# A further tile of an expert's tokens, placed between the main products of the next expert by an If/Else

## What is computed

```python
s = jax.nn.sigmoid((t @ w_router).astype(jnp.float32))      # 384 tokens x 16 experts
... top group of 4 experts by its two best scores, top 2 experts inside it, weights w normalised
hid = jax.nn.silu(jnp.einsum('td,edf->tef', t, w_gate)) * jnp.einsum('td,edf->tef', t, w_up)
hid = hid * gates.astype(hid.dtype)[:, :, None]
out = jnp.einsum('tef,efd->td', hid, w_down)                # D = 1024, d_ff = 512
```

## Time and profile before

| | us |
|---|---|
| median of three runs | 1125.43 (1115.67 to 1126.11) |
| span of the profiled execution | 1121.9 |
| PE busy | 982.3 (88%) |
| DVE busy | 404.9 (36%) |
| ACT busy | 157.1 (14%) |
| POOL busy | 123.3 (11%) |
| read from HBM / written | 305.88 MB / 21.30 MB |

### The profile page before, as it was taken

How to read it: one execution, slowest core, us unless ns; L and a number is a source line. 1 busy time by engine, 2 the same in 40 slices (tenths; PEclk the granted TensorE clock), 3 DMA queues, 4 the chain that set the end, 5 groups by cost and what they waited for, 6 DMA issues and landing times. The chain is left out here.

```text
span 1121.9 us, 12453 instructions
## 1 busy us (share of the span) xinstructions
PE 982.3 (88%) x4812; PEld 467.2 (42%) x4812; DVE 404.9 (36%) x902; ACT 157.1 (14%) x364; POOL 123.3 (11%) x188
## 2 busy tenths in 40 slices
PE   4799999997898989988799979999678997889886
PEld 2555545454333333333266544554523333333332
DVE  0189855245211110111435994533521111011206
ACT  1101233220000000000130014422000000000010
POOL 1001200511000000000221020060200000000010
PEclk9899889997999999988799997999579999999988
DMA  9928973368999996999950475225965999999932
GB/s 339 383 95 310 302 298 108 124 219 355 424 420 425 425 367 272 422 427 421 360 220 24 150 270 223 76 92 185 362 234 220 415 426 425 423 424 422 420 134 75
DMA packets 64570, 328.59 MB, mean 293 GB/s; under 512 B 7448, under 2 KB 10184, under 8 KB 48084
## 3 DMA queue, kind: packets, MB, share of 16 engines
q1 hardware_dynamic: 44224, 277.89, 61.6%
q0 software_dynamic: 9072, 27.89, 6.8%
q10 hardware_dynamic: 11172, 21.42, 5.8%
HBM read 305.88 MB, written 21.30 MB: 292 GB/s over the span
## 5 line engine op out<-in xcount | busy, mean ns | idle before, releaser
L1782 PE MATMUL ps<-big 128*64 128x512 f32 x1024 | 244.6, 630 | 27.6 <-issue 11.9
L1798 PE MATMUL ps<-big,scr 128*64 128x512 f32 x624 | 156.3, 644 | 5.6 <-DVE scr L1428 4.3
L1477 PE MATMUL ps<-big 128*128 128x384 f32 (+2 forms) x448 | 147.9, 492 | 5.1 <-ACT big L786 5.1
L1782 PEld LDWEIGHTS ps<-big 128*64 128x64 f32 x1024 | 78.5, 144 | 173.1 <-issue 159.5
L1124 DVE SCALAR_TENSOR_TENSOR scr<-scr,convw 128x384 f32<-128x384 f32 x240 | 134.1, 613 | 2.3
L1441 DVE TENSOR_TENSOR scr<-ps,scr 128x256 f32<-128x256 f32 x32 | 13.6, 424 | 278.2 <-ACT scr L953 278.1
L1477 PEld LDWEIGHTS ps<-big 128*128 128x128 f32 x448 | 86.0, 193 | 64.7 <-issue 24.8
L1798 PEld LDWEIGHTS ps<-big,scr 128*64 128x64 f32 x624 | 50.6, 148 | 97.9 <-issue 96.9
L1698 PE MATMUL ps<-big 128*128 128x512 f32 x192 | 84.4, 594 | 1.4 <-ACT big L826 1.4
L1493 PE MATMUL ps<-big,cs_rep 128*32 128x256 f32 x640 | 49.5, 466 | 14.4 <-DMA big<-in_w_mod_dram 14.4
L953 ACT ACTIVATE scr<-ps 128x256 f32<-128x256 f32 x32 | 12.3, 383 | 325.2 <-PE ps L1782 325.2
(11 more groups left out here) (231 smaller groups left out, 842.5 us busy)
## 6 DMA issues: line engine op xcount, KB each, us to landing
big<-in_w_gate_dram SPq DMA_DIRECT2D x32, 2048.0 KB, 18.4
big<-in_w_up_dram SPq DMA_DIRECT2D x32, 2048.0 KB, 22.8
big<-in_w_down_dram SPq DMA_DIRECT2D x32, 2048.0 KB, 18.9
big<-in_w_mod_dram SPq DMA_DIRECT2D x23, 2048.0 KB, 15.3
big<-in_w_in_dram SPq DMA_DIRECT2D x6, 2048.0 KB, 23.5
expert_rows<-scr ACTq DMA_DIRECT2D x68, 128.0 KB, 8.5
big<-in_w_out_dram SPq DMA_DIRECT2D x4, 2048.0 KB, 19.8
expert_rows<-x ACTq DMA_DIRECT2D x1, 7168.0 KB, 42.6
```

The lines of the kernel that those rows point to most:

```text
L1477: mm = pe.matmul(out, stationary(k), moving(k), start=(k == 0), stop=(k == n - 1))
L1782: mm = pe.matmul(ps[b * TT:(b + 1) * TT, bank, :].rearrange("p (m n) -> p m n", m=2), tokens(k), w[:, :, k, b * HF:(b + 1) * HF], start=(k ...
L1798: mm = pe.matmul(ps[b * TT:(b + 1) * TT, bank, :], src[:, k % 2 * P + k // 2 * TT:k % 2 * P + (k // 2 + 1) * TT], w[:, k, b * SEG:(b + 1) ...
```

## The change

On every engine a further tile of expert e-1 moves into the step of expert e. The step is one If/Else on the number of tokens of e-1. In the If arm the tile's operations stand between the main ones; the Else arm holds the main ones alone. So the main operations stand in the program twice.

- PE, If arm: loop for tiles 2 to 5 (`far`), transposes of the tile, main gate/up of e, gate/up of the tile, main down of e-1, next `xT`, hidden transposes of the tile, of e, down of the tile.
- ACT and DVE follow in the same order. POOL gathers the tiles 2 to 5 first, then tile 1.
- Gate and up slots of e-1 are signalled by the first two matmuls of the main down (If) or of the main gate/up of e (Else); the down slot by a small matmul behind the tile's down (If) or the first hidden transpose of e (Else). ACT waits for a new semaphore `y_ps` of `down_main`.
- Experts 14 and 15 have arms of their own. With a further tile of 15, ACT and DVE take the main hidden rows of 15 and the first picked rows ahead of the tile's; without one the order is the old one. The sum with 15's further tile (`sums_15b`) stands behind all products.
- `ov_xsT_free` is new: it tells POOL that the second buffer of the last picked rows is free, where it waited for the copy of the tile's result (`ov_taken`).

The core of the diff, PE:

```diff
-                def expert(e):
...
-                    if past(g0):
-                        pe.wait_ge(hid_ready, g0)
...
-                    gate_up(GU, e, lambda k: hT[i % 2][:, k, j * TT:(j + 1) * TT]).then_inc(gu_ps, 1)
...
-                    if 0 < e < E - 1:
-                        down_main(e - 1)
-                    if j and e + 1 < E:
-                        pe.wait_ge(gathered[(i + 1) % 2], (l * (E // 4) + (i + 1) // 2 + 1) * 16)
-                        xT(i + 1)
-                    pe.wait_ge(hid_ready, g0 + 1)
-                    hidden_transposes(hid, HT).then_inc(hidT_ps, 1)
-                    if e < E - 1:
-                        overflow(pe, n, run, ov_at)
-                    for m in ("g", "u"):
-                        idle_matmul(OV_GU).then_inc(slot_used[slot_of((m, l, e))], 1)
+                for e in range(1, E - 1):
+                    n = tokens_of(pe, e - 1)
+                    with pe.If(n > TT):
+                        if e == 1:
+                            pe.wait_ge(last_taken, l + 1)
+                        far(e - 1, n)
+                        more_transposed(e - 1)
+                        gate_up_main(e)
+                        more_gate_up(e - 1)
+                        down_main(e - 1, slots_gu(e - 1))
+                        next_xT(e)
+                        more_hidden()
+                        hidden_main(e)
+                        more_down(e - 1)
+                        release(("d", l, e - 1))
+                    with pe.Else():
+                        gate_up_main(e, slots_gu(e - 1))
+                        if e == 1:
+                            pe.wait_ge(last_taken, l + 1)
+                        down_main(e - 1)
+                        next_xT(e)
+                        hidden_main(e, slot_used[slot_of(("d", l, e - 1))])
+                n = tokens_of(pe, E - 2)
+                with pe.If(n > TT):
+                    far(E - 2, n)
+                    more_transposed(E - 2)
+                    down_main(E - 2)
+                    more_gate_up(E - 2)
+                    more_hidden()
+                    more_down(E - 2)
+                    release(("g", l, E - 2))
+                with pe.Else():
+                    down_main(E - 2)
+                    release(("g", l, E - 2))
...
+                n = tokens_of(pe, E - 1)
+                with pe.If(n > TT):
+                    loaded(("g", l, E - 1))
+                    loaded(("u", l, E - 1))
+                    far(E - 1, n)
+                    more_transposed(E - 1)
+                    gate_up_main(E - 1)
+                    more_gate_up(E - 1)
+                    hidden_main(E - 1)
+                    pe.wait_ge(y_taken, l * E + E - 1)
+                    sums_14(0)
+                    more_hidden()
+                    down_main(E - 1)
+                    more_down(E - 1)
+                with pe.Else():
+                    gate_up_main(E - 1)
+                    pe.wait_ge(y_taken, l * E + E - 1)
+                    sums_14(0)
+                    hidden_main(E - 1)
+                    down_main(E - 1)
```

DVE for experts 1 to 14, and ACT and DVE for expert 15 with a further tile:

```diff
+                    with dve.If(n > TT):
+                        far_(e - 1, n)
+                        more_x()
+                        hid_of(e)
+                        more_hid(e - 1)
+                        if e % 2:
+                            take_xT(e // 2 + 1)
+                        more_hidT()
+                        hidT_of(e)
...
+                with act.If(n > TT):
+                    far(E - 1, n)
+                    sigmoid_of(E - 1)
+                    scale_pick(l, 0)
+                    scale_pick(l, 1)
+                    more_sigmoid(E - 1)
+                    take_y(E - 1)
+                    scale_pick(l, 2)
+                    more_y_kept()
...
+                    hid_of(E - 1)
+                    add_picked(l, 0)
+                    more_hid(E - 1)
+                    hidT_of(E - 1)
+                    more_hidT()
+                    add_picked(l, 1)
```

The new order of POOL, and its wait:

```diff
                     with pool.If(n > TT):
-                        run(1)
                         with pool.If(n > 2 * TT):
                             for t in range(2, NT):
                                 run(t)
-                        pool.reg_add(ov_at, ov_at, 0)
+                        run(1)
...
-                            pool.wait_ge(ov_taken if n else ov_x_free, asked)
+                            pool.wait_ge(ov_xsT_free if n else ov_x_free, asked)
```

More of the change, by code:

```diff
@@ new lines, in more_y_kept, with row_of, far @@
+                def more_y_kept():
+                    act.wait_ge(ov_y, act.snap(ov_at))
+                    a.copy(ov_y15, ps[:, OV, :]).then_inc(ov_taken, 1)
+                    act.reg_add(ov_at, ov_at, 1)
+                    act.reg_add(ov_next, ov_next, 1)
+                def row_of(e):
+                    return act.value_load(count[0:1, E + e:E + e + 1], min_val=E, max_val=E + MORE - NT + 1)
+                def far(e, n):
+                    def run(t):
+                        row = row_of(e)
+                        more_sigmoid(e)
+                        more_y(t, row)
+                    far_tiles(act, n, run, ov_at)
@@ new lines, in _ @@
+                sigmoid_of(0)
+                act.wait_ge(last_ps, l + 1)
+                for to, bank in ((T15, 6), (T14, OV), (T15b, OV_GU)):
+                    ins = a.copy(to.rearrange("p t n -> p (t n)"), ps[:, bank, 0:TILES * P])
+                ins.then_inc(last_taken, 1)
+                for e in range(1, E - 1):
+                    n = tokens_of(act, e - 1)
+                    with act.If(n > TT):
+                        far(e - 1, n)
+                        row = row_of(e - 1)
+                        sigmoid_of(e)
+                        more_sigmoid(e - 1)
+                        take_y(e - 1)
+                        more_y(1, row)
+                    with act.Else():
+                        sigmoid_of(e)
+                        take_y(e - 1)
@@ new lines, in _ @@
+                n = tokens_of(act, E - 2)
+                with act.If(n > TT):
+                    far(E - 2, n)
+                    row = row_of(E - 2)
+                    take_y(E - 2)
+                    more_sigmoid(E - 2)
+                    more_y(1, row)
+                with act.Else():
+                    take_y(E - 2)
+                n = tokens_of(act, E - 1)
+                with act.If(n > TT):
+                    far(E - 1, n)
[6 more added lines that the diff above has]
+                    more_y_kept()
@@ new lines, in more_hidden, with more_down, far, run @@
+                def more_hidden():
+                    pe.wait_ge(ov_hid_ready, pe.snap(ov_at))
+                    hidden_transposes(ov_hid, OV).then_inc(ov_hT, 1)
+                def more_down(e):
+                    loaded(("d", l, e))
+                    pe.wait_ge(ov_hidT_ready, pe.snap(ov_at))
+                    down(OV, e, ov_hidT).then_inc(ov_y, 1)
+                    pe.reg_add(ov_at, ov_at, 1)
+                    pe.reg_add(ov_count, ov_count, 16)
+                def far(e, n):
+                    def run(t):
+                        more_transposed(e)
+                        more_gate_up(e)
+                        more_hidden()
+                        more_down(e)
+                    far_tiles(pe, n, run, ov_at)
```

285 lines of the change are left out of this document (141 added, 144 removed).

## The result

| | before | after |
|---|---|---|
| median | 1124.13 us (1115.67 to 1126.11) | 1141.64 us (1138.14 to 1142.34) |
| ratio to before, 95% | 1 | 1.0181 (1.0139 to 1.0222) |
| span of the profiled execution | 1121.9 us | 1140.0 us |

The change made the kernel slower by 1.8% (by the two medians alone, 1.6%). The forecast was 1155 us in a range of 1109 to 1178: the direction and the mechanism, slow branches, came out, and the size was too large. Against the profiled spans +30 us were forecast and +18 measured.

What follows compares the result with a forecast made beforehand. Weight transfers (an expert every 16.4 us) bound the saturated stretches, TensorE others and the end. 1121.9 + 23 (layer 0) + 15 (layer 1) - 8 (last experts) = 1152, plus 3.5 from span to median: 1155 us, range 1109 to 1178.

Steps and rivals of the forecast that it cites:

- The branch: TensorE's jump over the If arm (377 or 392 instructions) often lands past the following packet; 6.5 and 7 slow branches.
- the branch behind an If arm: TensorE, step after one with a tile: reached while the tile's down still runs, so most of it is hidden.
- The price of a slow branch: TensorE, per slow branch: 4.59 us of delay plus 1.54 us of slowed product, 6.1 us.
- a DMA share under 1 late in both stages: Sign that the forecast is right: DMA share below 1 late in the expert stages of both layers.
- Layer 0, +23: Layer 0's expert stage: TensorE 507 us plus 6.5 x 6.1 = 39.7 ends at 547, 23 us later.
- What came after it in layer 0: Rest of layer 0 behind expert 14's hidden transposes: no term of its own, the 23 us kept in the sum.
- Layer 1, +15: Layer 1's expert stage: TensorE 1027 us plus 7 x 6.1 = 42.7 ends at 1069.7, 15 us later.
- The last two experts, -8: End of layer 1: first picked rows run beside TensorE, expert 15's down ends at about 1100, 8 us less.
- The tile between the main products, -4 and -2: Steps with a tile take 24.9 us instead of 29.0; saves about 4 us in layer 0, about 2 in layer 1.
- fetch stays hidden: Rival: the instruction stream holds the branch target at nearly every step; 14 us come off, 1111 us; chance 0.20.
- The slot signals at nothing: Weight slots signalled 1 to 2 us later starve nothing, as DMAs are four transfers behind; costed at nothing.
- the third rival, later slots: Later slot signals starve the transfers: adds 5 to 10 us, 1163; alone nothing; chance 0.62 together with the forecast.

Runs made afterwards that it cites:

- old_short: The kernel before without TensorE's loop for tiles 2 to 5, its Ifs at one place, jump 129 or 140: 1117.70 us, ratio 0.9993.
- new_short: The changed kernel without TensorE's loop for tiles 2 to 5, never-run instructions keeping its Ifs at one place, jump 264 or 277: 1113.29 us, ratio 0.9946.
- old_all_hit: The kernel before with never-run instructions added to put its branches where the target is held: 1121.52 us, ratio 1.0026.
- old_all_miss: The kernel before with 126 or 141 never-run instructions lengthening its jumps, Ifs placed where the target isn't held: 1190.77 us, ratio 1.0655.
- the experiment: new_short with the order of before for expert 15 with a further tile: 1122.07 us, ratio 1.0033.
- new_all_hit: The changed kernel with never-run instructions added to put the branches of experts 1 to 14 where the target is held: 1123.59 us, ratio 1.0029.
- mix: The changed kernel with the tile ahead of the main products for experts 1 to 14, in an If without Else, Ifs well placed: 1117.51 us, ratio 0.9995.

## Why the prediction was right, and where not

**The branch.** Right, by its own steps. The 23 branches that skip an arm have their median at 4475 ns (the row's 435 is over all 33); the idle times ahead of the main products put down to issue are 3.4 to 4.9 us behind the slow ones, and 7.6 in one case; the instruction queue moved 81 packets for the 82 forecast. Six full prices fell in layer 0 before expert 14 (6.5 assumed) and six in layer 1 (7 assumed). One reading was wrong: the branch behind an If arm was to be mostly hidden by the tile's down. The branch at 378.4 takes 5514 ns and leaves TensorE idle for 3.41 us, the one at 991.5 takes 4475 and leaves it idle for 7.59. At the border, where a part of the wait was to appear, the branch at 508 is fast, and the product behind it stops for 0.34 us. By the Trainium skill (Runtime: NRT & Kernel Launch, section Instruction fetch mechanics) a taken branch out of a two-block window waits for a DMA; the traces agree (347 ns at 508, 5736 at 527), and the 2048 instructions that the section gives TensorE are not what this trace shows.

**The price of a slow branch** was a little high. From the branch at 445.0 to the one at 513.6 lie four steps of 17.2 us each on average; without a slow branch a step was 12.0. That is 5.2 us, not 6.1. The instruction queue moved two packets for each such step:

```profile
q1 hardware_dynamic: 3031, 32.90, 93.1%
q8 instruction: 10, 0.16, 0.7%
```

(445 to 530, five steps.) The weights' queue is as full here as in the earlier trace rows: 387 GB/s. A slow step of 17.2 us lies so close to the transfers' 16.4 that the sign forecast for the evidence, a DMA share under 1 late in both stages, hardly appeared: it is 1.00 from 445 to 530. Only stretches with a tile show it.

**Layer 0, +23.** The number is right, +22.7 to the branch behind hidden 14, and in part by luck, for two errors cancel. The sum let TensorE reach hidden 14 at 507 without slow branches and added 6.5 x 6.1 = 39.7 us. But no run with fast branches gets there by 507: hidden 14 ends at 521.6 in old_short and at 527.0 in new_short, where TensorE waits mostly for up weights. It ends at 546.1 in the kernel after, so the slow branches added 19 to 25 us, and not 39.7.

**What came after it in layer 0** is the step that was wrong. The sum ended layer 0's term at hidden 14 and carried its 23 us through the rest of the layer unchanged. The runs show 8.5 of them coming back there. It is tempting to put this down to the branch behind hidden 14, slow before and fast after, but the table above rules that out: old_short has it fast and is as long as old_all_hit (307.9 against 308.9 us), and old_all_miss has it slow and is as short as the kernel after (302.4 against 302.8). In before its wait lies beside the picked rows, which end later anyway: product 15 is done at 552.0, and DVE takes its hidden rows only at 555.1, behind the sums of the picked rows. What gave 7.7 of the 8.5 us back is that the store and the pick took 14.4 instead of 22.1 us. A delay ahead of a part must be followed to what ends that part, which here is not TensorE.

**Layer 1, +15.** It measured +12.9. The five branches from 1012.2 to 1062.3 include three under 0.5 us, one of 1.1 and one of 2.8 us, and TensorE caught up with the transfers at the end: expert 14's product, at 1068.64, waits 3.62 us for its up weights.

**The last two experts, -8.** Right: -9.4 in the two traces, 8.8 by the medians of the experiment and 4.0 by its traces. Both down products of 15 end at 1125.7, 44.9 us behind hidden 14 (1080.78), where the count gave 19.4 + 25 (the first row is hidden 14, the second holds the down products of the main and the further tile):

```profile
1080.78 0.50 PE L1855 MATMUL ps<-table_sb,scr 128*128 128x128 f32 x2
...
1118.60 7.09 PE L1864 MATMUL ps<-big,scr 128*64 128x512 f32 x32
```

**The tile between the main products, -4 and -2.** The step of a tile is about as short as counted (23.5 us in an even step, 26.1 in an odd one, for the counted 24.9; the terms of that count add up to 25.3 for an odd step), but the gain isn't there. In the kernel after the idle stretch of the transfers from 400 to 440 is as large as before, and with nearly all branches fast new_short has a layer 0 that is 4.6 us longer than that of old_short, and the same layer 1. That the tile now waits for the next expert's weights is what the traces show at expert 4; that this is all of it wasn't shown. So the rival "fetch stays hidden" had too fast a time as well: it said 14 us off, and new_short, the nearest to it, is 6 us below before.

**The slot signals at nothing.** Not contradicted at 1 to 2 us, nor measured; the third rival, later slots, shows only when the delay is 7 us, and then costs 6 to 10.

The sum, then: 0.3 + 22.7 - 8.5 + 12.9 - 9.4 = 18.0 us, for the forecast's 23 + 15 - 8 = 30. Of the 12 between them, 8.5 are the part behind hidden 14 of layer 0, 2.1 layer 1, 1.4 the end.

## What to carry to other kernels

In this kernel a branch that skips a long body cost by where its target lies among the packets of the instruction stream: count instructions, put the place and the jump of each branch beside the packets of the instruction queue, and do so for the old program as well as the new, since any edit moves all places behind it. Work duplicated into both arms of an If makes the jump longer for the path that takes neither; where steps last about as long as two fetches (12 us and some 6 us each here), keep the body that is usually skipped short. Before a slow branch is priced, look at what else ends the same stretch: the four of before cost at most some 4 us together, since TensorE then waited for the weights or the picked rows instead. For the same reason a delay doesn't travel unchanged to the end. And where transfers set the pace, an order that ties extra work to the next load's arrival gives away the time in which that work was free.

## What the runs showed of the hardware

- TensorE's branches come in kinds: 70 to 85 ns not taken, mostly 0.2 to 0.5 us taken with the target held, 1.5 to 3 us at places where the following packet's transfer falls beside the branch (2478 ns at 334.0 of after), and mostly 5.5 to 6.7 us where the target is past the following packet (3.4 to 4.9 at several places; why less there isn't shown). The most in these traces is 7.3 us.
- Crossing a border in sequence isn't free either if a jump came shortly before: 0.2 to 2.9 us of idle time inside a product, in new_all_hit, new_short and mix.
- After an idle time of 4.12 us the granted clock was 0.50 in the next 2 us, and the product there took 1.4 us more (8.46 instead of 7.09).
- 128 instructions that never run changed the time of this kernel by 49 us.
- A slow branch of some 6 us cost the whole kernel 2.7 us in the new order and 3.6 in the old one; the rest lay beside transfers.
- Open: some branches at good places are slow all the same (6.2 us at 489.9 of old_all_hit, 5.4 at 929.2 of mix). The instruction queue moved no packet in the 8 us ahead of each. What decides when a packet is requested isn't settled here.
